# One 128-column tile for index keys, index heads and gate columns, with the keys' second copy made by a transfer, and transposes of probabilities placed ahead of the levels

## The reference, cut to what matters

```
z = h @ w_in                                   # h: 256 x 1024, w_in: 1024 x 5720
(aq, ak, av, iq, ik, iw, gq, gk, gv, gr, ga, mga, mgb) = split(z)
#  ik: 64 columns (index keys), iw: 8 (weights of the index heads), ga: 16 (gate rank)
sc   = einsum('bqhd,bsd->bqhs', iq, ik)        # 8 index heads, all against the same 64-wide keys
I    = einsum('bqh,bqhs->bqs', iw * scale, relu(sc))   # chooses the 64 keys of each query
prob = softmax(logits of the chosen keys);  oa = prob @ v
glog = log_sigmoid(ga @ gla_gate_w2 + gla_gate_b) / 16 # decays of the linear attention
ob   = gla_chunked(gq, gk, gv, glog)
```

## Time and profile before

| | us |
|---|---|
| median of three runs | 1207.19 (1206.47 to 1207.97) |
| profiled execution, its own time | 1208.47 |
| profiled execution, span from first to last instruction | 1206.7 |
| PE busy in it | 1185.8 (98%) |
| DVE busy | 816.2 (68%) |
| ACT busy | 592.8 (49%) |
| mean granted clock of PE | 0.997 |

### The profile page before, as it was taken

One profiled execution on the slowest core, in us unless ns is written; L12 is line 12 of the kernel. 1 busy time (PEld: TensorE's weight loads), 2 busy tenths in 40 slices (PEclk: granted clock), 3 DMA queues, 4 the chain that ended last, 5 costly groups with the idle time before them and its releaser, 6 DMA issues.

```text
span 1206.7 us, 23415 instructions
## 1 busy us (share of the span) xinstructions
PE 1185.8 (98%) x10226; PEld 1157.8 (96%) x10226; DVE 816.2 (68%) x919; ACT 592.8 (49%) x669; POOL 131.8 (11%) x137
## 2 busy tenths in 40 slices
PE   6999999999999999999999999999999999999997
PEld 6999999998999999999999999999899999999996
DVE  4766645687978666654767665558799777666545
ACT  5644344555655544444544443446466454444443
POOL 2000001011521100001120000100134020000011
PEclk9999999999999999999999999999999999999998
DMA  7655555545345465555456565553544456656550
GB/s 265 221 199 192 192 193 189 166 152 180 136 141 193 165 223 197 194 191 189 161 183 227 187 205 183 198 184 140 210 140 141 146 174 214 201 184 207 178 175 36
DMA packets 33158, 218.77 MB, mean 181 GB/s; under 512 B 5248, under 2 KB 5664, under 8 KB 7072
## 3 DMA queue, kind: packets, MB, share of 16 engines
q1 hardware_dynamic: 33056, 217.27, 53.0%
HBM read 216.21 MB, written 1.05 MB: 180 GB/s over the span
## 4 chain that ended last, share of the span: by engine, by line
PE 93%; DVE 3%; ACT 1%; DMA 1%; issue 1%; SPq 0%; POOL 0%; POOLq 0%; DVEq 0%; ACTq 0%
PE psum L363 30%; PE psum L364 29%; PE psum L365 29%; PE psum L612 1%; DMA raw<-in_weights 1%; PE psum L490 1%; ACT w_hi L786 1%; DVE w_lo L1139 1%; PE psum L578 1%; PE psum L594 1%; PE psum L408 0%; PE psum L638 0%; DVE hB_lo L1466 0%; DVE hB_lo L1160 0%; DVE gates L1485 0%
## 5 line engine op out<-in xcount | busy, mean ns | idle before, releaser
L1139 DVE TENSOR_TENSOR w_lo<-raw,w_hi 128x2048 fp32r<-128x2048 f32 x201 | 460.1, 2292 | 221.5 <-ACT w_hi L786 221.5
L786 ACT ACTIVATE w_hi<-raw 128x2048 fp32r<-128x2048 f32 x201 | 385.2, 1917 | 378.4 <-PE psum L365 366.6
L363 PE MATMUL psum<-hA_hi,w_hi 128*128 128x256 f32 x1376 | 383.7, 279 | 0.0
L364 PE MATMUL psum<-hA_hi,w_lo 128*128 128x256 f32 x1376 | 380.2, 276 | 0.0
L365 PE MATMUL psum<-hA_lo,w_hi 128*128 128x256 f32 x1376 | 380.2, 276 | 0.0
L363 PEld LDWEIGHTS psum<-hA_hi,w_hi 128*128 128x128 f32 x1376 | 258.4, 188 | 3.1 <-issue 2.7
L364 PEld LDWEIGHTS psum<-hA_hi,w_lo 128*128 128x128 f32 x1376 | 258.4, 188 | 0.2
L365 PEld LDWEIGHTS psum<-hA_lo,w_hi 128*128 128x128 f32 x1376 | 258.3, 188 | 0.0
L363 PE MATMUL psum<-hB_hi,w_hi 128*128 128x256 f32 x832 | 232.5, 279 | 12.4 <-DVE w_lo L1544 10.0
L364 PE MATMUL psum<-hB_hi,w_lo 128*128 128x256 f32 x832 | 231.1, 278 | 0.0
L365 PE MATMUL psum<-hB_lo,w_hi 128*128 128x256 f32 x832 | 231.1, 278 | 0.0
(11 more groups left out here) (171 smaller groups left out, 1240.4 us busy)
## 6 DMA issues: line engine op xcount, KB each, us to landing
raw<-in_weights SPq DMA_DIRECT2D x203, 1024.0 KB, 4.8
x<-in_x SPq DMA_DIRECT2D x2, 512.0 KB, 6.0
raw<-in_weights SPq DMA_DIRECT2D x2, 512.0 KB, 7.9
out<-gates SPq DMA_DIRECT2D x4, 256.0 KB, 2.4
relu<-in_p SPq DMA_DIRECT2D x2, 256.0 KB, 5.3
consts<-in_consts SPq DMA_DIRECT2D x1, 448.0 KB, 11.7
gnorm<-in_gla_norm SPq DMA_DIRECT2D x2, 64.0 KB, 5.6
consts<-in_consts SPq DMA_DIRECT2D x1, 64.0 KB, 12.3
```

What stands on the lines that cost most here:

```text
L363: pe.matmul(o, lh, rh, start=start, stop=False)
L364: pe.matmul(o, ll, rh, start=False, stop=False)
L786: act.activation(w_hi[:, s, :], raw[:, s, :], ACT.Copy).then_inc(hi_ready[s], 1)
L1139: dve.tensor_tensor(w_lo[:, s, :], raw[:, s, :], w_hi[:, s, :].bitcast(F32), ALU.subtract).then_inc(lo_ready[s], 1)
```

## The change

The weights of the chunk `small` are packed anew on the host: one column tile of 128 (64 index keys, 8 head columns, 16 gate columns, 40 that nobody reads) takes the first half of the chunk, zeros the second. PE does 24 products for it in place of 48. The keys then stand once, on partitions 0 to 63 of `ikT[:, 1, :]`, with the heads on 64 to 71 and the gate columns on 72 to 87. SP copies the keys to partitions 64 to 127 of `ikT[:, 0, :]` by a transfer of 64 KB, issued between the loads of chunks MIX+7 and MIX+8 after a wait for DVE's `small`; PE waits for it ahead of the scores. `glog` reads rows 64 to 87. DVE scales 128x256 in place of 128x512. In the rounds, `turn_prob(j)` goes ahead of `level(j)`. POOL sets rows 64 to 87 of `w2` to zero after `ones` and `half_neg`, where it set `w2` first.

```diff
-GA_ROW = 8
+IW_ROW, GA_ROW, GATE_END = 64, 72, 88
-        w2 = sb("w2", [24, 256])
+        w2 = sb("w2", [P, 256])
+        keys_copied = sem("keys_copied")
                 for n in range(SLOTS, CHUNKS if last else CHUNKS + SLOTS):
+                    if n == SMALL + 6:
+                        wait_drained(sp, L, "small")
+                        wait_stands_alone(sp, sp_ticks)
+                        sp.dma_start(ikT[64:128, 0, :], ikT[0:64, 1, :]).then_inc(keys_copied, 16)
                     chunk(L, n)
...
-                chunk(SMALL, "small")
+                s = operands(L, SMALL)
+                wait_free(pe, L, "small")
+                wh, wl = (w[:, s, 0:1024].rearrange("p (k n) -> p k n", n=P) for w in (w_hi, w_lo))
+                for k in range(8):
+                    mm = three(bank[BANK_OF["small"]][:, 0:T], wh[:, k, :], wl[:, k, :], hA[0][:, k, :], hA[1][:, k, :], k == 0, k == 7)
+                mm.then_inc(chunk_done[s], 1)
...
+                pe.wait_ge(keys_copied, (L + 1) * 16)
                 for j in range(0, 8, 2):
                     if j < 4:
                         wait_drained(pe, L, f"iq{j // 2}")
-                    scores(iqT, lambda rows, hp, nk: ikT[rows, 0, 0:nk], "sc", j)
+                    scores(iqT, lambda rows, hp, nk: ikT[rows, 0 if rows.start else 1, 0:nk], "sc", j)
...
-                    mm = pe.matmul(bank[BANK_OF["glog"]][:, c * T:(c + 1) * T], w2[:, c * P:(c + 1) * P], ikT[0:24, 1, :],
+                    mm = pe.matmul(bank[BANK_OF["glog"]][:, c * T:(c + 1) * T], w2[IW_ROW:GATE_END, c * P:(c + 1) * P], ikT[IW_ROW:GATE_END, 1, :],
                                    start=True, stop=True)
...
+                    turn_prob(j)
                     level(j)
-                    turn_prob(j)
...
-            pool.memset(w2[:, :], 0.0).then_inc(w2_zeroed, 1)
             pool.memset(ones[:, :], 1.0).then_inc(ones_ready, 1)
             pool.memset(half_neg[:, :], -0.5).then_inc(half_ready, 1)
             pool.wait_ge(half_ready, 1)
+            pool.wait_ge(ones_ready, 1)
+            pool.memset(w2[IW_ROW:GATE_END, :], 0.0).then_inc(w2_zeroed, 1)
+            pool.wait_ge(w2_zeroed, 1)
...
-                take(L, "small", ikT[:, :, :])
+                name = "small"
+                dve.tensor_tensor(ikT[:, 1, :], bank[BANK_OF[name]][:, 0:T], rb[:, :], ALU.mult).then_inc(drained[BANK_OF[name]], 1)
...
-    small = [columns(w_in, COL["ik"], 64), columns(w_in, COL["ik"], 72), columns(w_in, COL["ga"], 120)]
-    mix = [rows(w_in, 4 * i, 512, COL["av"]) for i in range(2)] + [np.concatenate(small, axis=2)]
+    small = np.concatenate([columns(w_in, COL["ik"], 72), columns(w_in, COL["ga"], 56)], axis=2).reshape(P, 1024)
+    mix = [rows(w_in, 4 * i, 512, COL["av"]) for i in range(2)] + [np.concatenate([small, np.zeros_like(small)], axis=1)]
```

More of the change, by code:

```diff
@@ L321, in layer @@
                 sp.dma_start(gains[:, 1:5, :], a["gains"][L, :, 1:5, :]).then_inc(layer_landed, 16)
-                sp.dma_start(w2[GA_ROW:GA_ROW + 16, :], a["gla_gate_w2"][L]).then_inc(layer_landed, 16)
+                sp.dma_start(w2[GA_ROW:GATE_END, :], a["gla_gate_w2"][L]).then_inc(layer_landed, 16)
                 sp.dma_start(gbias[:, :], a["gla_gate_b"][L].rearrange("(c p) -> p c", p=P),
@@ L865, in mix @@
                 wait_filled(act, L, "wi")
-                act.activation(wi[:, :, :], bank[BANK_OF["wi"]][:, 0:2 * P].rearrange("p (t c) -> p t c", t=2)[:, :, 0:8], ACT.Copy,
+                act.activation(wi[:, :, :], bank[BANK_OF["wi"]][:, 0:2 * P].rearrange("p (t c) -> p t c", t=2)[:, :, IW_ROW:GA_ROW], ACT.Copy,
                                scale=float(64 ** -0.5 * 8 ** -0.5)).then_inc(drained[BANK_OF["wi"]], 1)
```

## The result

The changed kernel has a median of 1200.92 us (1199.1 to 1203.0, six runs) beside 1206.83 us of the kernel before (1206.04 to 1207.98, six runs). The ratio is 0.9944, with a 95% interval from 0.9934 to 0.9954: 6.8 us less, between 5.6 and 8.0. The two medians themselves are 5.9 us apart, a ratio of 0.9951, which lies in that interval. Forecast were 7.5 us and 1199.7, with a range from 1198.6 to 1202.8; 1200.92 is 0.2 above the forecast's own narrower range, in the part that was given to the first rival. The profiled execution took 1202.17 us with a span of 1200.4, 6.3 us under the span before.

The account below looks back on a forecast made before the run. PE was taken to bound the kernel, busy 1185.8 of 1206.7 us. Half a chunk less, 5.4, plus the transposes' order, 2.1, gave 7.5 us: 1207.2 to 1199.7, range 1198.6 to 1202.8, own narrower range 1198.7 to 1200.7.

Parts of the forecast that it names:

- the first rival: Transposes in the rounds stall for `prob_ready` or ACT's copy of earlier transposes: 1201.8 to 1203.6 us; chance 0.17.
- Half a chunk less: In `small`, 24 products fewer at 0.1134 us each: 2.72 us saved a layer, 5.44 us for two.
- The supply: Behind `small`, `w_lo` is ready 2.8 us early for `iq0` and 3.4 us early for `iq1`; no cost.
- The copy: SP's 64 KB copy of the keys lands in 5.6 us, hidden by 3.0 us ahead of the first scores.
- The bound of 8.6 us: Landing time of the keys' copy beyond which PE begins to wait ahead of the first scores.
- the price beyond the bound: Late copy, PE waits at first scores: 1199.7 + 2 x (landing - 8.6) us; chance 0.05 still paying, 0.03 slower.
- Transposes ahead of the levels: In the rounds, `turn_prob(j)` before `level(j)` saves changes of PE's tile: 1.05 us a layer, 2.1 us for two.
- What the order does to the others: In the rounds, `turn_prob(j)` waits for `normalise(j)` about 1.0 us earlier; tightest is round 6, with 1.2 us left.
- the price of the changes of tile: On PE in the rounds, each change costs 0.10 us at its step and 0.05 to 0.11 at the next.
- The others: In the rounds, DVE's slack absorbs PE's gain; `level(j)` ends 0.2 to 0.45 us later, moving POOL's `klev` at most that.
- double step: Rival: the 24 products of `small` or those behind step up to twice as long: 1205.1 us; chance 0.05.
- The sign that was to warn of this: A wait of PE for DVE's `prob` in the rounds would show the prediction wrong; none was expected.

Follow-up runs that it names:

- e1: The changed kernel with the old order in the rounds, `level(j)` ahead of `turn_prob(j)`: 1201.3 us, ratio 0.9950 to the kernel before.
- e4: The changed kernel with DVE's `normalise(1)` moved behind the update of the states: 1200.69 us, ratio 0.9940 to the kernel before.
- e7: The changed kernel with the copy of the keys two loads later in SP's order: 1213.84 us, ratio 1.0048 to the kernel before.

## Why the prediction was right, and where it wasn't

**Half a chunk less: right.** 5.44 us forecast, 5.44 measured, from e1 alone and from both layers of each kernel with the new tile. The supply held: no `w_lo` is waited for in the mixer.

**The copy: right in its size.** 5.6 us of landing taken, 5.0 to 5.2 measured; the keys lie ready 3.5 to 3.7 us early, where 3.0 was forecast. The bound of 8.6 us fits as well: from the issue at 210.93 to the first scores at 219.62 are 8.7. What the price beyond the bound, one us a layer for each us of lateness, left out is the clock: behind a wait of 4.5 us it was at half during nearly all of the scores in the first layer and most of them in the second, which cost 2.5 and 1.6 us more.

**Transposes ahead of the levels: the sign right, the size wrong, 2.1 us forecast and 0.6 measured.** Two steps of the sum failed.
The larger is in "What the order does to the others". It asked whether `prob_ready` and ACT's copy of the previous transposes would be there, and found the tightest place in round 6. `turn_prob(j)` also waits for its bank, and in round 0 the previous user of bank 4 is not a transpose but U0, the product that the states are made from, which DVE frees at the end of its state update, at 290.93 in the trace before, 0.5 us behind mg0's last product at 290.43. The level had covered that. The wait costs 0.53 us and a longer step behind it 0.03, turns a gain of 0.35 into a loss of 0.21, and makes 1.1 us of the missing 1.5. e4 removes it without touching the order. The first rival had the right kind of event, a stall for DVE at the transposes, but another place; in round 6, where it was expected, nothing waits.
The smaller is the price of the changes of tile in rounds 1 to 6: 0.70 us a layer forecast, 0.52 measured. Rounds 2 and 4 were given the 0.35 of round 0. Counted as the sum did, from the last product of a chunk to the second of the next, round 2 goes from 305.04 to 308.52 before and from 301.56 to 304.77 now:

```profile
305.04 0.28 PE L365 MATMUL psum<-hA_lo,w_hi 128*128 128x256 f32 x1
305.24 1.11 PE L612 MATMUL psum<-qlev,klev 64*128 64x64 f32 x16
306.28 0.44 PE L578 MATMUL psum<-consts,prob 128*128 128x128 f32 x2
306.65 1.14 PE L490 MATMUL psum<-kT,qT 64*128 64x256 f32 x8
307.71 0.32 PE L594 MATMUL psum<-probT,v 128*64 128x128 f32 x1
...
308.52 0.28 PE L364 MATMUL psum<-hA_hi,w_lo 128*128 128x256 f32 x1
...
301.56 0.28 PE L370 MATMUL psum<-hA_lo,w_hi 128*128 128x256 f32 x1
301.68 0.38 PE L589 MATMUL psum<-consts,prob 128*128 128x128 f32 x2
301.99 1.11 PE L623 MATMUL psum<-qlev,klev 64*128 64x64 f32 x16
302.94 1.08 PE L495 MATMUL psum<-kT,qT 64*128 64x256 f32 x8
303.95 0.32 PE L605 MATMUL psum<-probT,v 128*64 128x128 f32 x1
...
304.77 0.28 PE L369 MATMUL psum<-hA_hi,w_lo 128*128 128x256 f32 x1
```

That saves 0.27, and round 4 saves 0.29. The logits were credited with 0.10 for their second step, measured on round 0's narrower ones; here they go from 1.06 us to 1.01. The other parts came within 0.02 of what was taken. By the same count the odd rounds lose their forecast 0.05 (round 1 goes from 1.64 to 1.69) and round 6 gains its forecast 0.15 (3.08 to 2.93), and round 0 alone, with its wait gone, gives 0.34. The last hundredths of the 0.18 lie in the steps within the chunks.
The rule of the Trainium skill, TensorEngine Tiling (Array Packing), Key Properties, that a change of mode drains TensorE, fits here: all the gain sits in rounds with fewer changes, and odd rounds, with as many as before, gain nothing. Priced with the 0.10 us step alone, an estimate, it had given 1.4 us; with its wait gone the whole order gives 0.83 us a layer (e4), 1.7 in all, between that and my price. That the changes of tile set the price is read from these steps; what PE does during one, no run shows.

**The others: right.** DVE's full rounds took nothing back from rounds 1 to 6, and POOL's and ACT's later levels delayed nobody. No tile ran at double step.

**The sum.** 5.44 + 0.61 is 6.05 us from the segments, within the interval of the times. The forecast's 7.5 lies in that interval too, but 1.5 us of it weren't there: that 6.8, the difference by the ratio, comes so near to it is the spread of the times and not the sum. The sign that was to warn of this, a wait of PE for `prob`, did not show by its letter; the wait at the transposes is for their bank.

## What to carry to other kernels

When an instruction is moved ahead in its queue, list every semaphore it waits for, the release of its output buffer too, and look up who had that buffer before it in the first turn of the loop; it may be another stage's tile. Where PE is solid, the price of small products is in the changes of tile shape between them, so order them by shape, but only in those rounds where a change really falls away. A transfer that PE waits for wants its place in the queue checked in units of loads ahead of it: here one load more was still hidden, with 0.1 us to spare in one layer, and two cost 12 us.

## What the runs showed of the hardware

- A wait of PE of 4.5 to 4.6 us ahead of the scores cost 7.0 us in the first layer and 6.2 in the second. The granted clock was at half (0.50) from 222.1 to 228.9 us in the first, falling while PE stood, and from about 819.5 to 822.9 in the second, falling about 0.5 us after PE had come back (e7). The kernel before has no such wait inside the mixer.
- A transfer of 64 KB within the core's memory, issued 0.4 us behind a 1 MB load on the same queue, landed after 5.0 us, about when that load did (5.2 us from its own issue). In all profiles it took 4.8 to 5.6 us.
- Segments of PE without waits repeat to 0.03 us between kernels, runs and layers, while whole times of one kernel spread over 3 to 4 us. In the eleven profiles the spread sits outside them, at the start above all: PE's first product came between 7.9 and 10.7 us, its steps shortened from 0.21 to 0.12 us between 12.2 and 16.1 us, and `small` began between 203.65 and 207.21. What lies between the two mixers differs by up to 0.9 us, the tail by up to 0.6.
